# Turning attention outputs over one PSUM bank with five open outputs, and zero-padded compressed operands

## The reference, cut to what matters

```python
# first block
h = rmsnorm(x); dq, dk, dv, sq, sk, sv = split(h @ w_qkv)
mix = concat([diff_attention(dq, dk, dv), stick_breaking(sq, sk, sv)]) @ w_o
x = x + rmsnorm(mix)
x = x + rmsnorm(conv_geglu_ffn(rmsnorm(x)))
# second block
h = x + 0.5 * swiglu(rmsnorm(x))
h = h + hybrid_mixer(rmsnorm(h))        # compressed + selected + window attention, and a 128-wide window
h = h + 0.5 * swiglu(rmsnorm(h))
return rmsnorm(h)
# inside the mixer: 31 compressed keys and values (kc, vc) for each of 2 groups of 4 heads
s = einsum('btgrd,bcgd->bgrtc', q, kc) * SCALE - slope * dist ; p_cmp = softmax(s) (masked)
o_cmp = einsum('bgrtc,bcgd->btgrd', p_cmp, vc)
```

## Time and profile before

| | us |
|---|---|
| median of 3 runs | 1716.87 (1716.31 to 1727.45) |
| the profiled execution | 1714.23 |
| its span | 1712.4 |
| PE busy | 1670.4 (98%) |
| DVE, ACT, POOL busy | 700.0, 697.6, 780.6 |

### The profile page before, as it was taken

One profiled execution on the slowest core, in us unless ns is written; L12 is line 12 of the kernel. 1 busy time (PEld: TensorE's weight loads), 2 busy tenths in 40 slices (PEclk: granted clock), 3 DMA queues, 4 the chain that ended last, 5 costly groups with the idle time before them and its releaser, 6 DMA issues.

```text
span 1712.4 us, 21609 instructions
## 1 busy us (share of the span) xinstructions
PE 1670.4 (98%) x8248; PEld 1381.2 (81%) x8248; DVE 700.0 (41%) x1400; ACT 697.6 (41%) x1230; POOL 780.6 (46%) x594
## 2 busy tenths in 40 slices
PE   9999989999999999999999999999989999999997
PEld 7877777888888887888888888888877888888885
DVE  6366743884444227212222245554552321112224
ACT  5366744543334225322223234665462322223222
POOL 7335524464444551744445545342011464444550
PEclk9999989999999999999999999999879999999999
DMA  5411102222222222222322222221001222222221
GB/s 197 145 46 50 50 1 98 99 98 99 96 94 94 99 98 84 89 99 98 99 98 98 93 93 99 87 75 38 14 26 62 91 95 98 98 99 98 99 97 51
DMA packets 42118, 147.39 MB, mean 86 GB/s; under 512 B 4768, under 2 KB 5152, under 8 KB 42016
## 3 DMA queue, kind: packets, MB, share of 16 engines
q1 hardware_dynamic: 40536, 143.13, 24.7%
q10 hardware_dynamic: 1480, 2.89, 0.5%
HBM read 142.84 MB, written 3.41 MB: 85 GB/s over the span
## 4 chain that ended last, share of the span: by engine, by line
PE 90%; DVE 4%; ACT 3%; issue 2%; POOL 1%; DMA 1%; DVEq 0%; ACTq 0%; POOLq 0%
PE PS L483 20%; PE PS L484 20%; PE PS L485 20%; PE PS L1119 5%; PE PS L1108 5%; PE PS L938 4%; PE PS L914 3%; PE PS L459 3%; PE PS L929 2%; PE PS L465 1%; PE PS L505 1%; PE PS L507 1%; PE PS L506 1%; DVE H_lo L441 1%; DVE L L1022 1%
## 5 line engine op out<-in xcount | busy, mean ns | idle before, releaser
L527 POOL TENSOR_TENSOR w_lo<-stage,w_hi 128x512 fp32r<-128x512 f32 x524 | 710.8, 1382 | 721.4 <-ACT w_hi L515 720.7
L515 ACT ACTIVATE w_hi<-stage 128x1024 fp32r<-128x1024 f32 x262 | 274.8, 1056 | 507.1 <-DMA stage<-in_weights 506.7
L483 PE MATMUL PS<-H_hi,w_hi 128*128 128x512 f32 x992 | 387.7, 391 | 0.4 <-DVE rcol L1289 0.4
L485 PE MATMUL PS<-H_hi,w_lo 128*128 128x512 f32 x992 | 385.9, 389 | 0.0
L484 PE MATMUL PS<-H_lo,w_hi 128*128 128x512 f32 x992 | 385.9, 389 | 0.0
L483 PEld LDWEIGHTS PS<-H_hi,w_hi 128*128 128x128 f32 x992 | 186.2, 188 | 40.4 <-issue 1.0
L484 PEld LDWEIGHTS PS<-H_lo,w_hi 128*128 128x128 f32 x992 | 186.2, 188 | 39.2 <-issue 1.0
L485 PEld LDWEIGHTS PS<-H_hi,w_lo 128*128 128x128 f32 x992 | 186.2, 188 | 38.7
L483 PE MATMUL PS<-A_hi,w_hi 128*128 128x512 f32 x528 | 205.6, 389 | 0.2
L484 PE MATMUL PS<-A_lo,w_hi 128*128 128x512 f32 x528 | 205.4, 389 | 0.0
L485 PE MATMUL PS<-A_hi,w_lo 128*128 128x512 f32 x528 | 205.4, 389 | 0.0
(11 more groups left out here) (239 smaller groups left out, 2225.6 us busy)
## 6 DMA issues: line engine op xcount, KB each, us to landing
stage<-in_weights SPq DMA_DIRECT2D x262, 512.0 KB, 3.2
out_t<-Y SPq DMA_DIRECT2D x8, 256.0 KB, 2.0
X<-in_x_t SPq DMA_DIRECT2D x3, 512.0 KB, 8.5
bias_line<-bias_line ACTq DMA_DIRECT2D x1, 1270.0 KB
strip<-bias_line ACTq DMA_DIRECT2D x1, 1024.0 KB, 5.1
stage<-in_weights SPq DMA_DIRECT2D x2, 256.0 KB, 4.3
X<-in_x_t ACTq DMA_DIRECT2D x2, 256.0 KB, 5.5
V<-QF SPq DMA_DIRECT2D x4, 128.0 KB, 2.5
```

Source lines behind the costliest of these rows:

```text
L483: pe.matmul(out, a, h_hi, start=first, stop=False, skip_group_check=skip)
L485: return pe.matmul(out, b, h_hi, start=False, stop=last, skip_group_check=skip)
L515: act.activation(w_hi[:, slot, :], stage[:, slot, :], ACT.Copy).then_inc(hi_done, 1)
L527: lo = pool.tensor_tensor(w_lo[:, slot, cols], stage[:, slot, cols], w_hi[:, slot, cols].bitcast(F32), ALU.subtract)
```

## The change

It does these things in one edit:

- Turns use bank 7 alone. Turn g waits for the split (lo part) of turn g-1 and not of g-2, and the first of block one for the evacuation of bank 7 (count 16 and not 15). The DVE part hangs one step earlier, at ACT's step.
- Bank 6 is free, so 5 outputs are open. They are taken in the order `WO_ORDER = [6, 0, 1, 2, 3, 4, 5, 7]`. The first takes group g-1 right after turn g is issued, inside the attention. Chunks 1 and 2 of that order follow in the last steps, chunks 3 and 4 after the attention with the turns of groups 6 and 7 behind them. Then groups 6 and 7 are multiplied for the 5 open ones, and 3 chunks are done whole.
- The compressed keys of both groups stand in one 128x64 tile with zeros beside them (`kc2`), so one product of 128 rows x 64 columns serves both; the values stand in a 128x512 tile (`vc4`, in QF) with zeros, so one product of 128 rows x 256 columns gives all 4 token blocks of a head. 32 products become 16, and 32 become 8. Their softmax hooks move by some steps.
- `pe_first` of the last FFN begins with three units and does the fourth after them (`late=1`), and the norm before it goes through the chunks in the new order.

The diff, cut to its core:

```diff
+WO_ORDER = [6, 0, 1, 2, 3, 4, 5, 7]
+EARLY = 5
+WO_NEXT = {1: (1,), 3: (2,), 4: (3,), 5: (4,), 6: (5, 6)}
...
-FILL2 = FILL2 + [4] * 6 + [0] * 6 + [(0, 12), (12, 12), 12]
+FILL2 = FILL2 + [(0, 4), 0] + [(0, 4), (3, 0)] * 5 + [(3, 12), (12, 6), 6]
...
-FILL1 = ([7] * 8 + [8] * 4) * 2 + [7] * 8 + [8] + [6] * 8 + [4] * 6 + [0, (0, 12), (12, 12), 12]
+FILL1 = ([7] * 8 + [8] * 4) * 2 + [7] * 8 + [8] + [6] * 8
+FILL1 = FILL1 + [(0, 4)] * 2 + [(3, 4)] * 4 + [(3, 0), (3, 12), (12, 6), 6]
+def turn_steps(g):
+    return 4 * (g + 1) + 3 * max(0, g - 1)
...
-        def pe_first(pe, n, u0, units):
+        def pe_first(pe, n, u0, units, late=0):
+            for part in ([range(units - late), range(units - late, units)] if late else [range(units)]):
+                pe.wait_ge(lo_done, u0 + part[-1] + 1)
+                for k in range(KC):
+                    pe.wait_ge(n.hi, k + 1)
+                    c = n.order[k]
+                    for j in part:
...
-            pe_first(pe, norm, u_up, 4)
+            pe_first(pe, norm, u_up, 4, late=1 if norm is n_ffn2 else 0)
...
         def pe_turn1(pe, b, g):
-            k, bank = TURN_ORDER[b][g], 6 + g % 2
+            k, bank = TURN_ORDER[b][g], 7
...
-            if g >= 2:
-                pe.wait_ge(o_split[b], g - 1)
+            if g >= 1:
+                pe.wait_ge(o_split[b], g)
             else:
-                pe.wait_ge(qk_evac[b], 15 + g if b == 0 else len(EVAC2))
+                pe.wait_ge(qk_evac[b], 16 if b == 0 else len(EVAC2))
...
         def pe_wo_early(pe, b, a):
-            for g in range(6):
+            yield from pe_turn1(pe, b, 0)
+            for g in range(1, 6):
                 yield from pe_turn1(pe, b, g)
+                if g == 1:
+                    pe.wait_ge(lo_done, (U_WO, U_WO2)[b] + 1)
+                yield from pe_wo1(pe, b, 0, [g - 1])
+            yield from pe_wo1(pe, b, 0, [5])
             pe.wait_ge(a.s_read, sum(len(it.maps) for it in a.items))
-            for j in range(EARLY):
-                pe.wait_ge(lo_done, (U_WO, U_WO2)[b] + j + 1)
-                if j == 3:
-                    pe.wait_ge(a.wt_ready, len(a.items) - 1)
-                yield from pe_wo1(pe, b, j, range(6))
+            for at in range(1, 3):
+                pe.wait_ge(lo_done, (U_WO, U_WO2)[b] + at + 1)
+                yield from pe_wo1(pe, b, at, range(6))
...
         def pe_wo_rest(pe, b, a):
+            for at in range(3, EARLY):
+                pe.wait_ge(lo_done, (U_WO, U_WO2)[b] + at + 1)
+                if WO_ORDER[at] == 3:
+                    pe.wait_ge(a.wt_ready, len(a.items) - 1)
+                run(pe_wo1(pe, b, at, range(6)))
+                run(pe_turn1(pe, b, at + 3))
             for g in (6, 7):
-                for _ in pe_turn1(pe, b, g):
-                    pass
-                for j in range(EARLY):
-                    for _ in pe_wo1(pe, b, j, [g]):
-                        pass
-            for j in range(EARLY, KC):
+                for at in range(EARLY):
+                    run(pe_wo1(pe, b, at, [g]))
+            for at in range(EARLY, KC):
...
-            hook(at1, "dve0", at + 1, lambda dve, g=g: dve_turn1(dve, 0, g))
+            hook(at1, "dve0", at, lambda dve, g=g: dve_turn1(dve, 0, g))
...
+        def dve_blank_values(dve):
+            dve.memset(kc2[:, :], 0.0).then_inc(cm["none"], 1)
+            dve.wait_ge(cm["pre_t"], 1)
+            dve.memset(vc4, 0.0).then_inc(cm["none"], 1)
...
+        def pe_cmp_s(half):
+                pe.wait_ge(cm["kv_sb"], 6)
+                if half == 1:
+                    pe.wait_ge(cm["z"], 4)
+                for r in (2 * half, 2 * half + 1):
+                    for i in range(TB):
+                        mm = pe.matmul(PS[:, 7, bass.ts(4 * (r % 2) + i, 64)], QF[:, 2 + r, bass.ts(i, P)], kc2[:, :],
+                                       start=True, stop=True)
...
+        def pe_cmp_pv(pair):
+                for h in (2 * pair, 2 * pair + 1):
+                    mm = pe.matmul(PS[:, 7, bass.ts(h % 2, 256)], cmp_PT(h), vc4[:, bass.ts(h // 4, 256)], start=True, stop=True)
...
-            hook(at2, "dve", at + 8 + 4 * g, dve_cmp_shift(g))
-            hook(at2, "dve", at + 10 + 4 * g, dve_cmp_probs(g))
-            hook(at2, "dve", at + 11 + 4 * g, dve_cmp_weigh(g))
-            hook(at2, "pe", at + 13 + 4 * g, pe_cmp_turn(g))
+            hook(at2, "dve", at + 10 + g, dve_cmp_shift(g))
+            hook(at2, "dve", at + 12 + g, dve_cmp_probs(g))
+            hook(at2, "dve", at + 13 + g, dve_cmp_weigh(g))
+            hook(at2, "pe", at + 14 + 2 * g, pe_cmp_turn(g))
...
             act_turn1(act, 1, 6)
+            act_next(act, U_WO2)
             act_turn1(act, 1, 7)
-            for j in range(KC):
-                act_fold(act, n_ffn2, j)
-                act_next(act, U_WO2 + j)
+            for at in range(KC):
+                act_fold(act, n_ffn2, at)
+                for u in WO_NEXT.get(at, ()):
+                    act_next(act, U_WO2 + u)
+            act_next(act, U_WO2 + KC - 1)
```

More of the change, by code:

```diff
@@ L115, in unit_order @@
             order += list(range(16, 20))
-    order += list(range(24, U_MIX))
+    order += [24 + j for j in WO_ORDER] + list(range(U_UP1, U_MIX))
     order += [U_MIX + MIX_AT[name] for name in MIX_FIRST]
@@ L119, in unit_order @@
     order += [U_MIX + (17 + CMP_AT[name] if name in CMP_AT else MIX_AT[name]) for name in FILL2_TASKS]
-    return order + list(range(U_WO2, N_UNITS))
+    return order + [U_WO2 + j for j in WO_ORDER] + list(range(U_UP3, N_UNITS))
 MIX_AT = {n: i for i, n in enumerate(("q0", "q1", "q2", "q3", "ks", "kw", "kc", "vc",
@@ L349, in build, with __init__ @@
         class Norm:
-            def __init__(self, name, at, kind, src, before=None, stay=()):
-                self.name, self.at, self.src, self.before, self.stay = name, at, src, before, stay
+            def __init__(self, name, at, kind, src, before=None, stay=(), order=range(KC)):
+                self.name, self.at, self.src, self.before, self.stay, self.order = name, at, src, before, stay, order
                 self.total = rstd[:, :] if before is None else conv[:, 0, 0, :]
@@ L450, in dve_norm @@
                 dve.wait_ge(norm_inverse, n.at)
-        def pe_first(pe, n, u0, units):
[L454 to L460, removed]
+        def pe_first(pe, n, u0, units, late=0):
[3 more added lines that the diff above has]
+                    pe.wait_ge(n.hi, k + 1)
+                    c = n.order[k]
+                    for j in part:
+                        for w in (w_hi, w_lo):
+                            pe.matmul(PS[:, j, :], w[:, (u0 + j) % RING, bass.ts(c, P)], H_hi[:, c, :],
+                                      start=(k == 0 and w is w_hi), stop=False)
             for j in range(units):
@@ L1090, in act_turn1 @@
             act.wait_ge(o_turned[b], g + 1)
-            act.activation(turned(b, g)[0], PS[:, 6 + g % 2, :], ACT.Copy).then_inc(o_hi[b], 1)
+            act.activation(turned(b, g)[0], PS[:, 7, :], ACT.Copy).then_inc(o_hi[b], 1)
         def dve_turn1(dve, b, g):
```

151 lines of the change are left out of this document (75 added, 76 removed).

## The result

The changed kernel takes **1679.44 us** (median of 4 runs, 1677.88 to 1682.24) against a median of 1721.74 us for the kernel before (4 runs on the same chips): ratio 0.9767, 95% interval 0.9735 to 0.9798. Run a second time, among the experiments, it gave 1681.09 us (5 runs) against 1715.04 us, ratio 0.9789 (0.9768 to 0.9810). The profiled execution took 1680.9 us with a span of 1678.9 us.

What follows compares the result with a forecast made beforehand. PE, busy 98% of the span, was taken as the bound. Terms -4.0 - 7.4 - 16.2 - 10 = -37.6, less 10 taken back, gave -27.6 from 1714.2, or 1686.6; plus 2.6 for the median, 1689 us; range 1674 to 1704.

Steps and rivals of the forecast that it cites:

- no low clock at all: Rival: the second attention has no low clock left, giving 1679 us; chance 0.17.
- 10 us taken back: Second attention: low clock expected to stay, one long stretch (7 us) and half of another (3 us), subtracted from the gain.
- Part one: Behind the last two turns of each block: wide matmuls cover PE's waits for the split, 2.8 us gone per block.
- Part two: Block one: 18 wide matmuls leave the end, nine charged in full, covered turn waits, 0.8 us wait added: -4.0 us.
- Part three: Compressed products: logits 4.1 us less, outputs 4.3 us less, 1 us of PE waits added: -7.4 us.
- Part five: Low clock ahead of the second attention's turns, 1192 to 1207 and 1237 to 1248: up to -10 us if it vanishes.
- Part four: End of second attention: steps 84 to 95 in 20.5 us, shorter output product, two waits gone: -16.2 us at full clock.
- Part six: Start of the last FFN: three-unit beginning avoids a 2.6 us PE wait for POOL's lo parts: 0, up to +2.
- One bank becomes the pace: Rival: each second-attention turn waits for the round PE, ACT, DVE; 12.5 us lost there, giving 1703 us; chance 0.06.
- Slower: Rival: thinned turn steps pull the clock down over steps 64 to 95, giving 1737 us; chance 0.04.
- Low clock as long as before: Rival: second attention's low clock lasts as long, only elsewhere, giving 1697 us; chance 0.13.

Runs made afterwards that it cites:

- experiment 9: Kernel before with only DVE's split of a turned group moved one step earlier, in both blocks: 1707.33 us, ratio 0.9963.
- experiment 11: Kernel before with the compressed products on zero-padded operands and DVE's split one step earlier, banks and outputs as before: 1694.56 us, ratio 0.9856.
- experiment 2: Kernel before with all of the change except the compressed products with their operands and hooks: 1692.79 us, ratio 0.9835.
- experiment 3: Changed kernel with the last FFN beginning with all four units (late=0): 1683.83 us, ratio 0.9778 to the kernel before.
- experiment 4: Changed kernel with block two's turns in six successive steps, three wide matmuls behind each: 1683.70 us, ratio 0.9796 to the kernel before.
- experiment 5: Changed kernel with the DVE softmax steps of the two compressed groups three steps apart, not adjacent: 1678.00 us, ratio 0.9764 to the kernel before.
- experiment 6: Changed kernel with block two's turns in every other step but no wide matmuls between them: 1685.99 us, ratio 0.9782 to the kernel before.
- experiment 8: Changed kernel with the compressed softmax's DVE steps spread and block one's turns one step later: 1679.64 us, ratio 0.9789 to the kernel before.
- experiment 1: Kernel before with only the compressed products, their operands and moved hooks from the change: 1704.15 us, ratio 0.9897.
- experiment 7: Kernel before with 72 useless 256-column matmuls added in steps 84 to 95 of the second attention: 1713.34 us, ratio 0.9962.

## Why the prediction was right, point by point

1689 was predicted, the time is 1679 to 1681, inside the range and nearer to the rival "no low clock at all" (1679) than to the forecast. The time lies just below the 1681 to 1695 that the prediction gave its own case. Against the 1716.87 it started from, 1689 is a ratio of 0.984; measured were 0.9767 and 0.9789. In the profiled pair, -33.5 us of span, the sum of the parts was -37.6 us with no low clock left and -27.6 us with 10 us taken back.

**Part one, waits behind the last two turns: right.** 2.8 us in each block are gone; the chain above has the turns between runs of 18 matmuls. Experiments 9 and 11 do not cover these turns and keep the waits in full, 2 x 1.4 us a block, whatever else gets better.

**Part two, block one: -4.0 predicted, -4.9 in the pair.** Its pieces hold. Waits between 205 and 290 us go from 3.8 + 2.8 + 1.9 + 1.5 to 2.3 + 2.2 + 0.4 us, 5.1 less, where the parts gave 4.1 less (the 0.7 us for ACT's H_hi stands at the end of this stage before as well, at 292.77 us, outside the window). The wait for bank 7 was put at 0.8 us above the 1.5 us wait that it replaces: it is 2.3 us. But over all profiles this stage is 286.1 to 290.0 us with the new code (changed kernel twice, and experiments 2 to 6 and 8) and 292.8 to 298.8 us with the old (before, and experiments 1, 7, 9 and 11). Their means are 288.7 and 295.4: -6.7 us. The profile from which I predicted was the shortest of the old ones. The spread within each kind goes with the low clock in 208 to 240 us: 0.50 from 224 to 240 us in experiment 1 (298.8), 0.89 from 216 to 232 us in experiment 4 (286.1). At the same mean clock over 208 to 240 us, 0.79, the old code takes 292.8 and 293.2 us (before, experiment 11) and the new 289.5 to 290.0 (experiments 2, 5, 6 and 8): 3.3 us less with the clock held equal.

**Part three, compressed products: -7.4 predicted, -4 to -5 found.** The logits came as predicted: 32 instructions, 16 of them up to the next start in 1.76 us, 0.11 each. The outputs were mis-sized a little. The timeline of PE in the changed kernel, logits and outputs, each with the next start:

```profile
1173.05 1.95 PE L1420 MATMUL PS<-kc,QF 128*128 128x64 f32 x16
1174.81 0.47 PE L1133 MATMUL PS<-H_hi,w_hi 128*128 128x512 f32 x1
...
1225.52 1.08 PE L1516 MATMUL PS<-QF,scratch 128*128 128x256 f32 x4
1226.53 0.39 PE L930 MATMUL PS<-B_hi,Q_hi 64*128 64x256 f32 x2
```
1.01 us for 4 is 0.25 each, against 0.215 assumed by halving the 512-column row: 16 x 0.035 = 0.6 us. The formula of the Trainium skill ("TensorE: Matmul & The Clock Gate", "Back-to-back issue gap") for an isolated matmul gives 109 ns at 256 columns, an estimate, and the section has no figure of its own for plain fp32; measured is more than twice that. The waits were the larger miss: PE waited 2.5 us for DVE and ACT between 1150 and 1256 us before, and 5.1 us between 1150 and 1240 us after, so 2.6 us were added where I put 1 (range 0 to 3). The burst of the two groups' shifts was named; it was priced too low. -4.1 - 3.7 + 2.6 is -5.2 us. From the stage itself: -11.0 us, less the 6.8 us by which its low clock got shorter (next point), is -4.2.

**Part five and the sum, the clock: the term that was mis-sized.** I took 10 us back for low clock that would stay. Counted in windows of 8 us, length x (1 - PEclk), the stage from 1168 us on lost 10.2 us before (1192 to 1208, 1232 to 1248) and loses 3.4 us after (1200 to 1208): 6.8 us came and 3.4 were kept. In the turn steps and the output product, where the rest of the 10 could still have fallen, the clock is 1.00 in every profile with the turns on one bank (the changed kernel twice, experiments 2 to 6 and 8). That puts -37.6 + 3.4 = -34.2 us against the measured -33.5. That this fits so well is in part luck: part three fell short by 2 to 3 us, and parts two and four came out 0.9 and 1.5 us better. The 10 us taken back, one long stretch and half of another, followed the longest stretches of before; what stayed was of the size of the shortest, 1237 to 1248, 11 us at 0.69, which is worth 3.4.

**Part four, end of the second attention: -16.2 predicted, -17.7 measured; the mechanism only half told.** The twelve steps take 19.3 us (20.5 predicted). PE is busy 18.93 of them and waits 0.2 us, so PE sets them, near the 19.8 us worked out for six pairs; the 0.7 added for DVE and ACT was not needed, though experiment 6 shows them close behind, at about 18. I credited the new order of turns with the whole shortening. Experiment 9 shows that 7.1 us of it come with the earlier split alone, and nearly all of that as clock: 27.9 x 0.42 = 11.7 us before, 20.8 x 0.08 = 1.7 us with it, both upper bounds, since PE also waits in them. Part four worked the steps out at the full clock and named it, but did not see that the split's place in DVE's order brings it. Experiment 7 shows the price of the low clock from the other side. The new order's own share of the steps is at most about 1.5 us, and experiment 9 still had up to 1.7 us of low clock there. Its larger share is in the product, 9.1 us shorter: 18 wide matmuls fewer behind the steps (4.1 us), the two covered waits (2.8) and a first stretch at full clock (1.9 predicted; the product of experiment 9, at 1.00, is 2.0 us shorter than before). Here the prediction had a slip: its six pairs hold 18 wide matmuls, but it took only 15 off the end, 3.4 us instead of 4.1.

**Part six, start of the last FFN: right.** 0.2 us of wait with three units, 2.7 us with four (2.6 predicted).

**The rivals.** "One bank becomes the pace" stands only as one wait of 1.1 us in the profile of experiment 4. "Slower", the clock pulled down by thinner turn steps, is refuted by the changed kernel (1.00 from 1208 to 1306 us) and by experiment 6, with still thinner ones. "Low clock as long as before" did not come with the whole change but did with a part of it: in experiment 9 a low stretch stands ahead of the turns, and of 9.1 us saved behind the first turn 1.6 were lost there and 3.5 in block one. "No low clock at all" is nearly what happened.

**What stays open.** Why the 8 us stretch at 1200 us comes in some kernels and not in others. It follows the DVE burst in the changed kernel twice and in experiments 3 and 6, but experiment 4, with the same code up to step 84, ran without it, and so did experiments 1 and 11, with the same burst; experiment 8, with the burst spread, still has 0.79 there. Why in experiment 9 the clock fell at 1224 us with PE busy all the time from 1200 us on. And why the clock of the turn steps stays up with the early split, when PE idles there nearly as long as before. I have rows for when it falls, none for the cause.

## What to carry to other kernels

Where PE makes an operand, two other engines split it, and PE needs it again, look at the cover between before you add buffers. First move the split to the earliest place in its engine's order, then put matmuls of another output between producer and user; here one bank was then enough, and the bank freed holds another open output. When an output product gets shorter, count at once what the next stage's weights need, here 2.8 us of POOL for each unit. And price low clock stretch by stretch: a split moved one step earlier made twelve steps 7 us shorter with PE idle almost as long, and one profile of the same edit lost 5 us again elsewhere. So look at several executions before the whole is called shorter.

## What was not expected of the hardware

- Adding matmuls made a kernel faster (experiment 7: over 8 us more work, ratio 0.9962): steps 84 to 95 ran at 1.00 instead of 0.58.
- Yet a stage with PE busy 14.76 of 18.50 us held 1.00 (experiment 6), and one with PE busy 32.00 of 32.00 us fell to 0.63 (experiment 9). In these rows the busy share of a stretch doesn't tell its clock.
- The length of the low stretches differs between executions of one kernel: mean clock 0.972 to 0.983 for the kernel before, and its times of 1712.6 to 1727.4 us go with it (0.983 in the shortest run, 0.973 and 0.972 in the two longest); the changed kernel's is 0.991 to 0.996 and its spread 1677.4 to 1682.4.
- A plain fp32 product of 256 columns is two instructions of 0.25 us each; an fp32r product of 512 columns is one of 0.23 us.
